# Splitting the three fp32r products of each weight tile into 272, 256 and 264 columns instead of three times 264, with a join of 8 columns per tile on VectorE

## The reference

```python
h = rmsnorm(x, norm_mix)
parts = jnp.split(h @ w_in, IN_SPLITS, axis=-1)          # u, b_gate, c_gate, 9 x q/k/v, gate_a, gate_b
conv_y, conv_state = causal_dwconv(c_gate * u, conv_prev, conv_mix_w)
branch_a = (b_gate * conv_y) @ w_conv_out
att, kv_states = attend(qs, ks, vs)                      # q and k rotated; three dilated windows, merged
branch_b = att.reshape(n, t, ATT_W) @ w_attn_out
x = x + (jax.nn.sigmoid(gate_a) * branch_a + jax.nn.sigmoid(gate_b) * branch_b) @ w_out
h = rmsnorm(x, norm_ffn)
up, gate = jnp.split(h @ w_ffn_in, 2, axis=-1)
gate, ffn_state = causal_dwconv(gate, ffn_prev, ffn_conv_w)
x = x + (jax.nn.silu(gate + ffn_conv_b) * up) @ w_ffn_down
```

## Time and profile before

| | |
|---|---|
| runs, median of 3 | 1523.7 us (1522.82 to 1524.02) |
| profiled execution, its time | 1521.96 us |
| its span | 1520.4 us |
| granted TensorE clock, mean | 0.997 |
| TensorE products, busy | 1505.6 us (99%) |
| weight loads (PEld), busy | 1502.7 us (99%) |
| VectorE, ScalarE, GpSimd, busy | 891.6 (59%), 686.7 (45%), 77.4 us (5%) |
| DMA | 308.64 MB, mean 203 GB/s |

### The profile page before, as it was taken

The page is one execution under the profiler, slowest core; times in us unless marked ns, Lnnn a source line. Parts: engine busy times, 40 slices in busy tenths (PEclk is TensorE's granted clock), DMA queues, the critical chain, the costliest instruction groups (busy, mean ns, idle before and its releaser), DMA issues.

```text
span 1520.4 us, 31542 instructions
## 1 busy us (share of the span) xinstructions
PE 1505.6 (99%) x12450; PEld 1502.7 (99%) x12450; DVE 891.6 (59%) x1056; ACT 686.7 (45%) x756; POOL 77.4 (5%) x144
## 2 busy tenths in 40 slices
PE   9999999999999999999999999999999999999997
PEld 8999999999999999999999999999999999999996
DVE  8646555656666445666666565664444665656564
ACT  7444444434545344444444444443333444444452
POOL 2000001001221000100000000000000000000000
PEclk9999999999999999999999999999999999999998
DMA  7867566557788866554677776775556566665552
GB/s 278 275 184 251 175 207 214 155 153 204 226 251 251 260 180 182 169 185 161 194 253 245 237 238 215 250 247 184 180 181 181 180 180 181 181 181 191 182 178 99
DMA packets 145160, 308.64 MB, mean 203 GB/s; under 512 B 10112, under 2 KB 10240, under 8 KB 144528
## 3 DMA queue, kind: packets, MB, share of 16 engines
q1 hardware_dynamic: 139120, 268.73, 56.7%
q0 software_dynamic: 5920, 38.12, 7.5%
HBM read 301.39 MB, written 26.38 MB: 216 GB/s over the span
## 4 chain that ended last, share of the span: by engine, by line
PE 98%; DVE 1%; DMA 0%; SPq 0%; ACT 0%; issue 0%; DVEq 0%
PE acc L971 32%; PE acc L972 32%; PE acc L973 32%; PE side L1064 1%; PE side L1043 1%; DMA raw<-w_in 0%; DVE yg L948 0%; PE side L1055 0%; PE side L1116 0%; DVE w_lo L581 0%; PE side L1030 0%; DVE r L623 0%; PE side L1169 0%; ACT w_hi L366 0%; PE side L1002 0%; SPq L316 0%
## 5 line engine op out<-in xcount | busy, mean ns | idle before, releaser
L581 DVE TENSOR_TENSOR w_lo<-raw,w_hi 128x1024 fp32r<-128x1024 f32 x503 | 614.7, 1231 | 514.6 <-ACT w_hi L366 512.5
L366 ACT ACTIVATE w_hi<-raw 128x1024 fp32r<-128x1024 f32 x503 | 529.9, 1058 | 730.7 <-PE acc L973 680.7
L971 PE MATMUL acc<-h_hi,w_hi 128*128 128x264 f32 x2872 | 821.5, 286 | 2.1 <-DVE w_lo L581 2.0
L972 PE MATMUL acc<-h_lo,w_hi 128*128 128x264 f32 x2872 | 816.7, 284 | 0.0
L973 PE MATMUL acc<-h_hi,w_lo 128*128 128x264 f32 x2872 | 816.3, 284 | 0.0
L971 PEld LDWEIGHTS acc<-h_hi,w_hi 128*128 128x128 f32 x2872 | 539.9, 188 | 3.2 <-issue 2.7
L972 PEld LDWEIGHTS acc<-h_lo,w_hi 128*128 128x128 f32 x2872 | 540.0, 188 | 0.1
L973 PEld LDWEIGHTS acc<-h_hi,w_lo 128*128 128x128 f32 x2872 | 540.0, 188 | 0.0
L971 PE MATMUL acc<-f_hi,w_hi 128*128 128x264 f32 x704 | 200.6, 285 | 0.0
L972 PE MATMUL acc<-f_lo,w_hi 128*128 128x264 f32 x704 | 200.2, 284 | 0.0
L973 PE MATMUL acc<-f_hi,w_lo 128*128 128x264 f32 x704 | 200.1, 284 | 0.0
(11 more groups left out here) (187 smaller groups left out, 869.4 us busy)
## 6 DMA issues: line engine op xcount, KB each, us to landing
raw<-w_in SPq DMA_DIRECT2D x183, 512.0 KB, 3.7
raw<-w_ffn_in SPq DMA_DIRECT2D x176, 512.0 KB, 4.3
raw<-w_ffn_down SPq DMA_DIRECT2D x88, 512.0 KB, 3.7
raw<-w_out SPq DMA_DIRECT2D x32, 512.0 KB, 4.0
s_kv<-cache POOLq DMA_DIRECT2D x16, 1020.0 KB, 8.8
raw<-w_conv_out SPq DMA_DIRECT2D x16, 512.0 KB, 5.2
raw<-w_attn_out SPq DMA_DIRECT2D x8, 512.0 KB, 3.7
s_kv<-cache POOLq DMA_DIRECT2D x8, 508.0 KB, 5.0
```

Source lines behind the costliest of these rows:

```text
L366: act.activation(w_hi[:, s % RING], raw[:, s % RING], ACT.Copy).then_inc(hi_ready, 1)
L581: dve.tensor_tensor(w_lo[:, s % RING], raw[:, s % RING], w_hi[:, s % RING].bitcast(F32), ALU.subtract).then_inc(lo_ready, 1)
L971: pe.matmul(out, w_hi[:, slot, k, cols], backwards(m_hi[:, kt + k, :]), start=first and k == 0, stop=False)
L972: pe.matmul(out, w_hi[:, slot, k, cols], backwards(m_lo[:, kt + k, :]), start=False, stop=False)
```

## The change

Hi and lo parts of a row of activations now lie side by side in one tile (`h_rows[:, k, 0, :]` and `h_rows[:, k, 1, :]`, and so for the other four). The new `tile_products` reads that row of 528 columns in three pieces. With w_hi first columns 256 to 527 (the samples' hi part, 8 columns, and the whole lo part, 264), 272 columns into `acc[:, m, 0:272]`; then with w_hi columns 0 to 255 (the prompt's hi part), 256 columns into `acc[:, m, 8:264]`; then with w_lo the hi part, 264 columns into `acc[:, m, 8:272]`. So the prompt's sums lie in columns 8 to 263, and the samples have two partial sums, in columns 0 to 7 and 264 to 271. `join` on VectorE copies the first to SBUF (L593 of the new file), adds it to the second in PSUM (L595) and then lets the old reader run, each step after a wait on the one before. Where ScalarE takes the tile (q and k), VectorE joins in a new `join_group`, and ScalarE waits for `joined`. The first chunk now runs through `tile_products` too. The number of products, of weight loads and of DMAs stays as it was.

```diff
@@ -42,6 +42,7 @@
 BATCH = 8
 PAST = 256
 T = SEQ + BATCH
+WIDE = T + BATCH
 EPS = 1e-6
 THETA = 10000.0
 SCALE = HEAD_DIM ** -0.5
@@ -131,8 +132,8 @@
         w_hi = place("w_hi", [P, RING, 2, GW], F32R)
         w_lo = place("w_lo", [P, RING, 2, GW], F32R)
         h_at = cursor[0]
-        h_hi = place("h_hi", [P, KT, T], F32R)
-        h_lo = place("h_lo", [P, KT, T], F32R)
+        h_rows = place("h_rows", [P, KT, 2, T], F32R)
+        h_hi, h_lo = h_rows[:, :, 0, :], h_rows[:, :, 1, :]
         rot_at = cursor[0]
         rot = place("rot", [P, 2, T])
...
@@ -404,10 +407,10 @@
             def rope_inputs(group, unit, wait):
 
                 for m in range(TILES):
-                    wait_tile(act, group, 2 * group, N_MODEL, m)
+                    act.wait_ge(joined, TILES * group + m + 1)
                     if m == 0 and wait:
                         act.wait_ge(roped, unit)
-                    act.activation(qraw[:, m, :], acc[:, m, 0:T], ACT.Copy).then_inc(psum_free, 1)
+                    act.activation(qraw[:, m, :], acc[:, m, BATCH:WIDE], ACT.Copy).then_inc(psum_free, 1)
                 wait_taken(act, group, TILES - 1)
                 for dst, src in ((0, 64), (64, 0)):
                     act.activation(qswap[dst:dst + 64, :, :], qraw[src:src + 64, :, :], ACT.Copy).then_inc(swapped, 1)
@@ -585,6 +588,21 @@
                 for s in range(s0 + AHEAD, s1 + AHEAD):
                     lo(quad, s)
 
+            def join(group, m):
+
+                dve.tensor_copy(first_part[:, m, :], acc[:, m, 0:BATCH]).then_inc(part_copied, 1)
+                dve.wait_ge(part_copied, TILES * group + (m + 1))
+                dve.tensor_tensor(acc[:, m, T:WIDE], acc[:, m, T:WIDE], first_part[:, m, :], ALU.add).then_inc(joined, 1)
+                dve.wait_ge(joined, TILES * group + (m + 1))
+
+            def join_group(group, quad, s):
+
+                def joined_tile(m):
+                    wait_tile(dve, group, quad, s + 1, m)
+                    join(group, m)
+
+                take_tiles(joined_tile, quad, s)
+
             def take_tiles(take, quad=None, s=None):
 
                 for m in range(TILES):
@@ -649,7 +667,9 @@
                     for q in range(4):
                         lo(quad, RING + 1 + q)
                         sum_squares(sq0[:, 4 * q:4 * q + 4, :], 0, q)
-                    los(quad, RING + 5 - AHEAD, STATS_CHUNK)
+                    los(quad, RING + 5 - AHEAD, N_MODEL - 1)
+                    join_group(3 * g, quad, N_MODEL - 1)
+                    los(quad, N_MODEL, STATS_CHUNK)
                     row_factor(0)
                     los(quad, STATS_CHUNK, STATS_CHUNK + 1)
...
@@ -890,7 +923,8 @@
 
                 def take_gate_group(m):
                     wait_tile(dve, g, quad, N_MODEL, m)
-                    dve.tensor_tensor(fz[:, m, 2:2 + T], acc[:, m, 0:T], r[:, :], ALU.mult).then_inc(psum_free, 1)
+                    join(g, m)
+                    dve.tensor_tensor(fz[:, m, 2:2 + T], acc[:, m, BATCH:WIDE], r[:, :], ALU.mult).then_inc(psum_free, 1)
 
                 take_tiles(take_gate_group, quad, N_MODEL - 1)
...
@@ -958,19 +993,23 @@
 
                 return rows[:, ::-1]
 
-            def chunk(quad, s, group, first, last, m_hi, m_lo, kt):
+            def tile_products(m, slot, k, row, first, last):
+
+                row = row.rearrange("p a t -> p (a t)")
+                w1, w2 = (w[:, slot, k, m * P:(m + 1) * P] for w in (w_hi, w_lo))
+                pe.matmul(backwards(acc[:, m, 0:WIDE]), w1, backwards(row[:, SEQ:2 * T]), start=first, stop=False)
+                pe.matmul(backwards(acc[:, m, BATCH:T]), w1, backwards(row[:, 0:SEQ]), start=False, stop=False)
+                return pe.matmul(backwards(acc[:, m, BATCH:WIDE]), w2, backwards(row[:, 0:T]), start=False, stop=last)
+
+            def chunk(quad, s, group, first, last, rows, kt):
 
                 pe.wait_ge(lo_ready, 4 * quad + s + 1)
                 slot = s % RING
                 for m in range(TILES):
                     if first:
                         pe.wait_ge(psum_free, TILES * group + m + 1)
-                    cols = slice(m * P, (m + 1) * P)
-                    out = backwards(acc[:, m, 0:T])
                     for k in range(2):
-                        pe.matmul(out, w_hi[:, slot, k, cols], backwards(m_hi[:, kt + k, :]), start=first and k == 0, stop=False)
-                        pe.matmul(out, w_hi[:, slot, k, cols], backwards(m_lo[:, kt + k, :]), start=False, stop=False)
-                        mm = pe.matmul(out, w_lo[:, slot, k, cols], backwards(m_hi[:, kt + k, :]), start=False, stop=last and k == 1)
+                        mm = tile_products(m, slot, k, rows[:, kt + k], first and k == 0, last and k == 1)
                     if last and m < TILES - 1:
                         mm.then_inc(tile_done, 1)
                 mm.then_inc(slots_free, 1)
@@ -981,20 +1020,17 @@
                     pe.wait_ge(done, 1)
                     pe.wait_ge(h_lo_ready, k + 1)
                     for m in range(TILES):
-                        cols = slice(m * P, (m + 1) * P)
                         if k == 0:
                             pe.wait_ge(psum_free, m + 1)
-                        pe.matmul(acc[:, m, 0:T], w_hi[:, 0, k, cols], h_hi[:, k, :], start=k == 0, stop=False)
-                        pe.matmul(acc[:, m, 0:T], w_hi[:, 0, k, cols], h_lo[:, k, :], start=False, stop=False)
-                        mm = pe.matmul(acc[:, m, 0:T], w_lo[:, 0, k, cols], h_hi[:, k, :], start=False, stop=False)
+                        mm = tile_products(m, 0, k, h_rows[:, k], k == 0, False)
                 mm.then_inc(slots_free, 1)
 
-            def run(quad, group, n, m_hi, m_lo, s0=0, ready=None, counts=None):
+            def run(quad, group, n, rows, s0=0, ready=None, counts=None):
 
                 for s in range(n):
                     if ready is not None:
                         pe.wait_ge(ready, counts[s])
-                    chunk(quad, s0 + s, group, s == 0, s == n - 1, m_hi, m_lo, 2 * s)
+                    chunk(quad, s0 + s, group, s == 0, s == n - 1, rows, 2 * s)
 
             def row_sums(norm):
```

More of the change, by code:

```diff
@@ L202, in trunk_program @@
         cursor[0] = mix_at
-        t_hi = place("t_hi", [P, KT, T], F32R)
-        t_lo = place("t_lo", [P, KT, T], F32R)
+        t_rows = place("t_rows", [P, KT, 2, T], F32R)
+        t_hi, t_lo = t_rows[:, :, 0, :], t_rows[:, :, 1, :]
         tf = place("tf", [P, 2, TILES, T])
@@ L757, in take @@
                     wait_tile(dve, i + GROUP0[name], 2 * i + QUAD0[name], N_MODEL, m)
-                    dve.tensor_tensor(tiles(out, 4 * i + m), acc[:, m:m + 1, 0:T], over_tiles(r[:, :], 1),
+                    join(i + GROUP0[name], m)
+                    dve.tensor_tensor(tiles(out, 4 * i + m), acc[:, m:m + 1, BATCH:WIDE], over_tiles(r[:, :], 1),
                                       ALU.mult).then_inc(psum_free, 1)
@@ L865, in take @@
                     wait_tile(dve, group, quad, n, m)
-                    dve.tensor_tensor(tiles(x, tile + m), acc[:, m:m + 1, 0:T], tiles(x, tile + m),
+                    join(group, m)
+                    dve.tensor_tensor(tiles(x, tile + m), acc[:, m:m + 1, BATCH:WIDE], tiles(x, tile + m),
                                       ALU.add).then_inc(psum_free, 1)
@@ L1008, in h_run @@
                         row_sums(stats)
[L1009 removed]
+                    chunk(quad, s0 + s, group, s == 0, s == N_MODEL - 1, h_rows, 2 * s)
             pe.wait_ge(ones_ready, 1)
@@ L1141, in _ @@
             for i in range(0, 4):
-                run(2 * i + QUAD0["w_out"], i + GROUP0["w_out"], N_MODEL, t_hi, t_lo,
+                run(2 * i + QUAD0["w_out"], i + GROUP0["w_out"], N_MODEL, t_rows,
                     ready=t_ready, counts=[s // 2 + 1 for s in range(N_MODEL)])
```

55 lines of the change are left out of this document (34 added, 21 removed).

## The result

The changed kernel takes **1556.16 us** (median of 4 runs, 1554.46 to 1556.54) against 1523.26 (4 runs, 1522.43 to 1524.02): a ratio of 1.0217, with a 95% interval from 1.0205 to 1.0229. It is 33 us slower. The prediction was 1496 with a range up to 1534: wrong in sign, and outside its range. The profiled execution took 1556.54 us, its span 1555.0.

A forecast was written before the change was run, and what follows sets the result against it. TensorE's stream of 264-column products, 121.3 ns apart, was taken as the bound. -39.5 (columns) + 10.5 (stalls) + 1.2 (VectorE late) = -27.8 us against 1521.96 gave 1494.2, 1496 us in the runs; range 1484 to 1534.

The forecast's parts named there:

- The columns: TensorE's main products: the new widths make one product in three cheaper, 9.8 ns x 4,032 = 39.5 us saved.
- shape (a): fp32r product price: charged in blocks of 32 columns, 264 as 288, 256 as 256; in full, chance 0.38.
- its half: fp32r products: blocks counted by place in memory, so only 2,016 triples gain, -19.8 us, 1512 us; chance 0.16.
- Shape (c): fp32r product price: a dearer column, 0.46 ns each, so the new widths gain TensorE nothing.
- straight in columns: fp32r products: price follows columns, or has a fixed addition; no gain, 1528.4 us; no-gain chance 0.36.
- The hand-overs: Tiles passed to the next group: joins of 0.39 us stall TensorE, 10.5 us under blocks of 32, 3.5 otherwise.
- ScalarE's groups: Six q and k groups, joined by VectorE and read by ScalarE in 0.39 us: no added stall, 0.
- Where VectorE was late already: Second-last take beside GpSimd's t_lo, +0.8 us, and the group after the second attn_out, +0.4: together 1.2 us.
- Layout: Addresses of hi and lo parts side by side: 0 expected, ends -16 and +33 us.
- The end: Last take before the final fp32 products: its join hidden in 0.86 us of cover, otherwise 0.39 us.
- no-gain case: TensorE's products gain nothing from the new widths: 1528.4 us, up to 1534 with a dear join; chance 0.36.
- hand-over rival: Joins at 0.51 us instead of 0.39 add 28 us of stalls, cancelling the saving; above 0.45 with gain, chance 0.10.

The follow-up runs named there:

- series: Kernel before plus runs of 24 fp32r products of 64 to 512 columns behind its last output: 120.0 ns a product at 264 columns.
- experiment 4: Also spelled half_join: products of before with each join's 8-column copy but without its add: 1533.08 us against 1523.34 for the kernel before, ratio 1.0066.
- experiment 5: Also spelled split_last: changed kernel with VectorE's split of weights moved behind tile 3's take, joins kept: 1536.15 us, ratio 1.0086 to the kernel before.
- joins_only: Kernel before, its products and layout kept, with the joins put in (the add takes zeros): 1553.06 us, ratio 1.0194 to the kernel before.
- no_join: Changed kernel without the joins' copy and add, so one partial sum is unused: 1531.08 us against 1522.83 for the kernel before, ratio 1.0056.

## Why the prediction was wrong

**What bounds the kernel** was read rightly: the distance between products, and no wait unless it reaches TensorE. Each part of the loss came in by one of those two doors.

**The columns: the step that failed first.** The prediction took shape (a), blocks of 32 columns, since "those extra 24 ticks need a cause", and gave it 0.54 with its half. Shape (c), the dearer column, is the nearest to the truth (series: 118.1, 120.0, 124.5 and 233.4 ns for 256, 264, 272 and 512 columns). The argument for (a) was a wish for a cause; no row favoured it, and the fp32 rows at hand spoke for cost by column (the eight records of the earlier trace rows are the two passes of four products, not eight products, which changes nothing in the working). The rival "straight in columns" named its sign: 256 columns at 117 ns or more. They came at 118 to 119 and 272 at 126. Even this rival was too kind, with 0 where the widths cost 8.3 us: in the series single widths lie off the straight line (264 is a good one), and in the kernel the split's triple takes 365.0 to 366.7 ns. The term was -39.5 and measured +8.3. The Trainium skill's rule (TensorE: Matmul & The Clock Gate, Back-to-back issue gap), straight in the columns, had the shape roughly right; its size (112.5 ns for 264) these runs don't show: 120.0 at best.

**The hand-overs: right mechanism, wrong size.** The sum had 10.5 us of stalls (3.5 without (a)) and 1.2 where VectorE is late; the joins cost 25.1. Four terms were missed or mis-sized:
- *The refill.* A tile that is late costs 0.1 us more, as its successor's load of weights is not ahead: 82 tiles, 8.7 us by starts of products. The working had lateness only. The row that shows it was among those read (behind the stand of 0.36 us the product's bar is 0.39 us long, not 0.29).
- *The step from add to take.* Taken as 0.195 us; it is 0.21 in the FFN and 0.33 in w_out, down_a, gate_a and the later two v groups, where an instruction of 0.07 us on registers, for the computed wait, stands between the two. A join there costs 0.53, not 0.39, beyond the 0.51 at which the prediction's own rival decides; down_a and w_out lost about 0.7 us a group, where 0.27 was reckoned.
- *ScalarE's groups: "0".* The working compared the length of the reads and never asked what VectorE is doing when tile 0 of the first group is done: its sums of squares. 4.6 us of stand. Copying alone brings 4.4 of it (experiment 4).
- *The clock.* Two stands, of 4.6 and 2.1 us, are followed by 0.50: 3.5 us more.

The sign that was named for all this, 5 to 15 us of idle time before L1000, came true (8.0 us in the products of h) while the joins cost 25: in the products' rows most of the lateness hides behind their bars.

That the joins cost most of this by where they stand, and not by their work on VectorE, is shown by experiment 5: same work, another order, 20 us back.

**Where VectorE was late already**: +1.2 predicted; the stand grew from 0.36 to 2.1 us and drew 1.5 us of slow clock. **Layout**: 0, right (1.000). **The end**: hidden, right; the last run of fp32 products (L1169, L1205 after) takes 1.94 us before and after, and the sum is taken 1.98 us after its start in both. **The range** reached to the no-gain case with a dear join, 1534; the hand-over rival had the size of the stalls about right (28 us), but only together with the gain that it cancels. That both could go wrong at once had no place in it: the no-gain case with that rival's 28 us gives 1528.4 + 28 = 1556, the measured time, though its parts are others (0 for the widths in place of 8.3).

In sum: 0 for the layout, 8.3 us for the widths, 25.1 for the joins on top, 33 in all.

## What to carry to other kernels

A cost that one row shows at one width says nothing of its shape: if a change rests on the shape, take the dullest one (a price by column) until rows of several widths speak for another. When an engine gets a task between a producer and a reader who was another engine, look up what it is doing at each of those moments; free on average is not free then. And where a stream of products is the bound, price a late tile at its lateness plus one exposed load of weights, and put anything long (here a split of 1.2 us) behind the takes that the stream waits for.

## What the runs showed of the hardware

- An fp32r product costs 0.455 to 0.468 ns a column (one column a tick would be 0.417), with a floor of 111.5 ns where the weights have 128 columns; 264 columns took 120.0 ns, 256 118.1, 272 124.5.
- For the same 264 columns the distance moves with where successive moving rows start within 256 bytes: 121.1 to 122.5 ns where they start unlike, 120.0 where alike, with exceptions (rows 256 columns apart, alike, 121.0; one row read again and again from a start of 16 or 24 columns, 124.1 and 122.5). For rows that start alike but have the split's three widths the rule doesn't hold (122.2). Making the starts alike gave 0.9% of the whole kernel.
- TensorE's granted clock was 0.50 behind stands of 4.6 and 2.1 us in the middle of a full stream, for 4 and 3 us; joins_only, half_join and split_last show it behind the same first stand (4.3 to 4.6 us), and no_join, which has no such stand, does not. A stand of 2.16 us near the start was followed by products 0.12 us apart, so the length of the stand alone doesn't decide; what does was not tried.
- The split's triple took 365.1 ns in the groups of gate_a in the change and 366.7 in the same groups of no_join, which issue the same products from the same addresses. Why it has two values stays open.
